# Norm weights and roots behind the transposes, and a dense gate and up with the rows stationary

## The reference

```python
h = rms_norm(x, attn_norm[i])             # x * rsqrt(mean(x^2) + eps) * gain
sb_q, sb_k, sb_v, df_q, df_k, df_v = split(h @ w_in[i])
sb = rms_norm(stick_breaking(sb_q, sb_k, sb_v), sb_out_norm[i])       # 8 heads of 64
df = rms_norm(differential(df_q, df_k, df_v) , diff_subln[i]) * (1 - lambda_init)   # 4 heads of 128
x = x + concat(sb, df) @ w_out[i]
h2 = rms_norm(x, ffn_norm[i])
x = x + (silu(h2 @ w_gate) * (h2 @ w_up)) @ w_down         # layer 0, 2816 hidden columns
x = x + moe(h2)                                            # layer 1, top 2 of 8 experts, 3584 each
return rms_norm(x, final_norm)                             # after both layers
```

## Time and profile before

| | us |
|---|---|
| median of three runs | 1455.23 |
| profiled execution, device time | 1451.91 |
| profiled execution, span | 1450.1 |
| PE busy | 1410.1 (97%) |
| DVE busy | 1128.7 (78%) |
| ACT busy | 932.1 (64%) |
| POOL busy | 47.9 (3%) |
| mean granted TensorE clock | 0.993 of full |

### The profile page before, as it was taken

The page is one execution under the profiler, slowest core; times in us unless marked ns, Lnnn a source line. Parts: engine busy times, 40 slices in busy tenths (PEclk is TensorE's granted clock), DMA queues, the critical chain, the costliest instruction groups (busy, mean ns, idle before and its releaser), DMA issues.

```text
span 1450.1 us, 19281 instructions
## 1 busy us (share of the span) xinstructions
PE 1410.1 (97%) x7417; PEld 1200.2 (83%) x7417; DVE 1128.7 (78%) x843; ACT 932.1 (64%) x742; POOL 47.9 (3%) x58
## 2 busy tenths in 40 slices
PE   7999999999999999999999999999999999999996
PEld 6877899988977788888888888888888888888885
DVE  5674554545674799988898898888888889889897
ACT  4454443434554577777777777777777777777775
POOL 0011000000011002000000000000000000000200
PEclk9999999999999999999999999999999999999999
DMA  8741796555542599999999999999999999999992
GB/s 307 258 146 58 282 354 222 183 194 162 172 146 62 199 356 395 393 398 394 389 376 392 384 365 384 394 357 397 383 370 387 382 380 373 385 397 357 396 395 104
DMA packets 190547, 450.61 MB, mean 311 GB/s; under 512 B 7529, under 2 KB 10638, under 8 KB 190494
## 3 DMA queue, kind: packets, MB, share of 16 engines
q1 hardware_dynamic: 188270, 442.43, 83.3%
q0 software_dynamic: 1936, 6.86, 1.3%
q10 hardware_dynamic: 288, 0.59, 0.1%
HBM read 431.49 MB, written 18.36 MB: 310 GB/s over the span
## 4 chain that ended last, share of the span: by engine, by line
PE 92%; DVE 3%; DMA 2%; ACT 1%; POOL 1%; SPq 1%; issue 0%; DVEq 0%
PE ps L511 86%; PE ps L852 2%; DMA raw<-in_w_in 1%; PE ps L608 1%; DVE hn L1178 1%; POOL hn L476 1%; DMA hn<-bias_scratch 1%; PE ps L632 0%; PE ps L810 0%; PE ps L655 0%; DVE aT_lo L1186 0%; DMA bias_scratch<-vrow 0%; DVE w_lo L350 0%; PE ps L821 0%; PE ps L597 0%
## 5 line engine op out<-in xcount | busy, mean ns | idle before, releaser
L350 DVE TENSOR_TENSOR w_lo<-raw,w_hi 128x2048 fp32r<-128x2048 f32 x401 | 914.9, 2291 | 208.9 <-ACT w_hi L345 208.1
L345 ACT ACTIVATE w_hi<-raw 128x2048 fp32r<-128x2048 f32 x401 | 768.0, 1917 | 314.4 <-PE ps L511 304.3
L511 PE MATMUL ps<-w_hi,xe_hi 128*128 128x512 f32 x896 | 244.7, 395 | 0.0
L511 PE MATMUL ps<-w_hi,xe_lo 128*128 128x512 f32 x896 | 240.0, 390 | 0.0
L511 PE MATMUL ps<-w_lo,xe_hi 128*128 128x512 f32 x896 | 239.9, 389 | 0.0
L511 PEld LDWEIGHTS ps<-w_hi,xe_lo 128*128 128x128 f32 x896 | 168.2, 188 | 35.9
L511 PEld LDWEIGHTS ps<-w_lo,xe_hi 128*128 128x128 f32 x896 | 168.2, 188 | 35.5
L511 PEld LDWEIGHTS ps<-w_hi,xe_hi 128*128 128x128 f32 x896 | 164.6, 188 | 31.6
L511 PE MATMUL ps<-w_hi,he_hi 128*128 128x512 f32 x448 | 120.6, 391 | 0.0
L511 PE MATMUL ps<-w_lo,he_hi 128*128 128x512 f32 x448 | 119.9, 389 | 0.0
L511 PE MATMUL ps<-w_hi,he_lo 128*128 128x512 f32 x448 | 119.8, 389 | 0.0
(11 more groups left out here) (220 smaller groups left out, 956.9 us busy)
## 6 DMA issues: line engine op xcount, KB each, us to landing
raw<-in_expert_w_gate SPq DMA_DIRECT2D x112, 1024.0 KB, 7.8
raw<-in_expert_w_up SPq DMA_DIRECT2D x112, 1024.0 KB, 8.0
raw<-in_expert_w_down SPq DMA_DIRECT2D x112, 1024.0 KB, 7.8
raw<-in_w_in SPq DMA_DIRECT2D x24, 1024.0 KB, 7.8
raw<-in_dense_w_gate SPq DMA_DIRECT2D x11, 1024.0 KB, 6.6
raw<-in_dense_w_up SPq DMA_DIRECT2D x11, 1024.0 KB, 8.2
raw<-in_dense_w_down SPq DMA_DIRECT2D x11, 1024.0 KB, 4.8
raw<-in_w_out SPq DMA_DIRECT2D x8, 1024.0 KB, 5.1
```

The source lines that it names most:

```text
L345: nc.scalar.activation(w_hi[:, n % SPL, :], raw[:, n % RAW, :], ACT.Copy).then_inc(hi_ready, 1)
L350: nc.vector.tensor_tensor(w_lo[:, n % SPL, :], raw[:, n % RAW, :], w_hi[:, n % SPL, :].bitcast(F32), ALU.subtract).then_inc(lo_ready, 1)
L511: return pe.matmul(o, stationary, moving, start=start, stop=stop, skip_group_check=True)
```

## The change

The transposes now read `xs`, the raw residual (`turn_x`). Its two halves of columns are added apart (`add_half`); the first half is turned before w_out's or down's last tile, the second behind it. Each column of the gain stands on a partition of the transposed copy (`gT`, itself transposed from the gain rows at the start), so ACT's copy and DVE's subtraction take it as their scale (`turned_x`, four operations of 128 x 256 a side for two of 128 x 512). The root of a row is applied to each product's output: to queries and keys through `rB` (the root spread over columns by one product with `diag`), to differential scores, values and the dense gate (as Silu's scale) and up by row. The head gains `gC` go the same way as `gT`; POOL's and DVE's multiplications of head rows go.

Dense gate and up go by rows, second half of the residual's columns last; the product of Silu and up is transposed on PE (`turn_dense`, 44 transposes) and copied as `hT_hi` and `hT_lo`. The router reads unscaled transposed rows, with `rw` times the gain (loaded at the start on SP's queue); the one-hot of the gather carries the root, and ACT scales the stored rows in the first expert block. The dummy matmuls of a run, 12, 9, 11, 9, 6 and 4 in the order of the program, become 8 and 16 at the start and 6, 6 and 4 in the router. Cut to its core:

```diff
-                sp.dma_start(g_sb[:].rearrange("p l d -> p (l d)"),
-                             sb_out_norm.rearrange("l d -> (l d)").partition_broadcast(P)).then_inc(small_in, 16)
-                sp.dma_start(g_df[:].rearrange("p l d -> p (l d)"),
-                             diff_subln.rearrange("l d -> (l d)").partition_broadcast(P)).then_inc(small_in, 16)
+                sp.dma_start(head_rows[0:DEPTH, 0:HD], sb_out_norm[:, :]).then_inc(small_in, 16)
+                sp.dma_start(head_rows[0:DEPTH, HD:2 * HD], sb_out_norm[:, :]).then_inc(small_in, 16)
+                sp.dma_start(head_rows[DEPTH:2 * DEPTH, :], diff_subln[:, :]).then_inc(small_in, 16)
+                sp.dma_start(rw[:], router_w[0].rearrange("(k p) e -> p k e", p=P)).then_inc(rw_in, 16)
...
-            norms = [attn_norm[0], ffn_norm[0], attn_norm[1], ffn_norm[1], final_norm]
-
-            def load_gain(m):
-                pool.wait_ge(rows_done[1], [None, 1, 3, 4, 6][m])
-                pool.dma_start(gain[:], norms[m].partition_broadcast(P)).then_inc(gain_in, 16)
-
+            pool.dma_start(gain[:], ffn_norm[DEPTH - 1].partition_broadcast(P)).then_inc(gain_in, 16)
...
-                pool.wait_ge(sbo_saved, l + 1)
-                pool.wait_ge(small_in, 16 * 2)
-                for t in range(TT):
-                    h = hn[:, t, 0:HALF].rearrange("p (h d) -> p h d", d=HD)
-                    nc.gpsimd.tensor_tensor(h, h, g_sb[:, l, :].unsqueeze(1).to_broadcast([P, SB_HEADS, HD]),
-                                            ALU.mult).then_inc(sb_rows, 1)
                 if l == 0:
-                    load_gain(2)
+                    pool.wait_ge(x_done[1], 1)
...
-            keep_running(12, 0)
+            keep_running(8, 0)
+            pe.wait_ge(norms_in, 32)
+            pe.transpose(ps[:, 3, 0:2 * DEPTH * KT], norm_rows[:], ident[0:2 * DEPTH * KT, 0:2 * DEPTH * KT]).then_inc(gT_turned, 1)
+            turn_x(0, (0, 1, 2, 3), 4)
+            keep_running(16, 0)
...
+                pe.wait_ge(diag_done, l + 1)
+                pe.matmul(ps[:, 6, 0:S], ones, diag[:].rearrange("p t k -> p (t k)"), start=True, stop=True,
+                          skip_group_check=True).then_inc(rB_spread, 1)
...
-                turn_rows(3 * l + 1, (0, 1), 6)
+                turn_rows((0, 1))
                 pe.wait_ge(t_lo, 12 * l + 8)
-                w_out(2)
-                w_out(3, ends=True)
-                keep_running(9, 6)
-                turn_rows(3 * l + 2)
+                w_out(2, ends=True)
+                w_out(3, (0,), ends=True)
+                turn_x(2 * l + 1, (0, 1))
+                w_out(3, (1,))
...
+                    def turn_dense(n):
+
+                        pe.wait_ge(hid_done, n + 1)
+                        width = CH if n < D_FULL else D_REST
+                        for f in range(width // P):
+                            for t in range(TT):
+                                last = pe.transpose(ps[:, 4 * (n % 2) + f // 2, (f % 2) * S + t * P:(f % 2) * S + t * P + P],
+                                                    hn[:, n % 2, t * width + f * P:t * width + f * P + P], ident)
+                        last.then_inc(hT_turned, 1)
...
+                        if n == 0:
+                            pe.wait_ge(t_lo, 10)
+                            rows_out(g, bank, 1, opens=1, tiles=(0,))
+                            turn_x(1, (2, 3))
+                            rows_out(g, bank, 1, opens=1, tiles=(1,))
+                            pe.wait_ge(t_lo, 12)
+                            rows_out(g + 1, bank, 0, opens=1)
+                        elif n < D_FULL:
+                            rows_out(g, bank, 1, opens=1)
+                            rows_out(g + 1, bank, 0, opens=1)
+                        else:
+                            rest_out(g, bank)
+                        if n > 0:
+                            turn_dense(n - 1)
                         if n < D_FULL:
-                            for half in range(2):
-                                if n == 0:
-                                    pe.wait_ge(t_lo, 10 + 2 * half)
-                                columns_out(g + half, bank, half)
-                            for half in range(2):
-                                columns_out(g + 2 + half, bank + 2, half)
+                            rows_out(g + 2, bank + 2, 1, opens=1)
+                            rows_out(g + 3, bank + 2, 0, opens=1)
                         else:
-                            columns_out(g, bank, 0, KT, D_REST)
-                            columns_out(g + 1, bank + 2, 0, KT, D_REST)
-                    for i in range(DENSE_DN):
-                        n = PROJ + WOUT + DENSE_GU + i
-                        hi = high(n)
-                        if i % 2 == 0:
-                            pe.wait_ge(hT_lo_done, i // 2 + 1)
+                            rest_out(g + 1, bank + 2)
...
+                            if (c, t) == (1, 1):
+                                turn_x(2, (0, 1))
+                            down_hi(DENSE_DN - 2, c, t)
+                            last = down_lo(DENSE_DN - 2, c, t)
...
+            pe.wait_ge(rw_ready, 1)
+            pe.wait_ge(rT_done, 2)
+            for k in range(4):
+                logits(k)
+            keep_running(6, 1)
+            turn_x(2 * DEPTH - 1, (2, 3))
+            pe.wait_ge(rT_done, 3)
+            for k in (4, 5):
+                logits(k)
+            pe.wait_ge(rT_last, 1)
+            logits(6)
+            logits(7).then_inc(lg_done, 1)
...
+            def turned_x(r, pairs, bank=6):
+
+                m, l = 2 * (r // 3) + r % 3 // 2, r // 3
+                for i, j in enumerate(pairs):
+                    act.wait_ge(t_done, 4 * r + j + 1)
+                    for q in range(2):
+                        k = 2 * j + q
+                        last = copy(aT_hi[:, x_slot(m, k), :], ps[:, bank + i, q * S:q * S + S], gT[:, DEPTH * (m % 2) + l, k:k + 1])
+                    last.then_inc(t_hi, 1)
...
-                    row_norms(0)
+                    act.wait_ge(gT_saved, 1)
+                    turned_x(0, (0, 1), 4)
                     split_hi(act, 0)
-                    turned(0)
+                    turned_x(0, (2, 3), 6)
                     split_hi(act, 1)
                     split_hi(act, 2)
+                    row_norms(0)
                 else:
+                    turned_x(3, (0, 1))
+                    split_hi(act, n0 + 1)
                     row_norms(2)
+                    turned_x(3, (2, 3))
                     split_hi(act, n0 + 2)
-                    turned(3 * l)
...
-                copy(both(v_sb[:]), both(ps[:, 0:2, :])).then_inc(v_sb_saved, 1)
-                turned(3 * l + 1, (2, 3), 6, 0)
+                act.wait_ge(r_done, 2 * l + 1)
+                for t in range(TT):
+                    last = copy(v_sb[:, t, :], ps[:, t, :], row_fine[:, t:t + 1])
+                last.then_inc(v_sb_saved, 1)
+                act.wait_ge(gC_saved, 1)
+                turned(3 * l + 1, (2, 3), gC[:, 1, l:l + 1])
...
+                    def silu(n):
+
+                        act.wait_ge(piece_used, min(PROJ + WOUT + 4 * n + 4, PROJ + WOUT + DENSE_GU))
+                        act.wait_ge(r_done, 2)
+                        for t in range(TT):
+                            at = slice(t * chunk(n) // TT, (t + 1) * chunk(n) // TT)
+                            last = nc.scalar.activation(hn[:, n % 2, at], both(ps[:, 4 * (n % 2):4 * (n % 2) + 2, :])[:, at],
+                                                        ACT.Silu, scale=row_fine[:, t:t + 1])
+                        last.then_inc(silu_done, 1)
...
+            def scale_rows():
+
+                act.wait_ge(ga_done, 2)
+                act.wait_ge(r_done, 4)
+                for t in range(TT):
+                    copy(hn[:, t, :], hn[:, t, :], row_fine[:, t:t + 1]).then_inc(rows_scaled, 1)
...
+            def low_part(out, source, gain_column, hi):
+                return V.scalar_tensor_tensor(out=out, in0=source, scalar=gain_column, in1=hi.bitcast(F32),
+                                              op0=ALU.mult, op1=ALU.subtract)
...
+                root(2 * l)
+                for t in range(TT):
+                    last = V.tensor_scalar(diag[:, t, :], ident, row_fine[:, t:t + 1], None, ALU.mult)
+                last.then_inc(diag_done, 1)
...
-                V.tensor_copy(both(qk_df[:, 4:8, :]), both(ps[:, 2:4, :])).then_inc(k_df_saved, 1)
+                V.tensor_tensor(qk_df[:, 4:8, :], four(ps[:, 2:4, :]), r_columns, ALU.mult).then_inc(k_df_saved, 1)
...
+                dve.wait_ge(piece_used, n0 + 6)
+                V.scalar_tensor_tensor(out=qk_sb[:, 0:4, :], in0=four(ps[:, 0:2, :]), scalar=HD ** -0.5, in1=r_columns,
+                                       op0=ALU.mult, op1=ALU.mult).then_inc(q_sb_saved, 1)
...
-                V.tensor_copy(both(v_df[:]), both(ps[:, 0:2, :])).then_inc(v_df_saved, 1)
```

(33 more changed lines are left out.)

484 lines of the change are left out of this document (302 added, 182 removed).

## The result

| | before | after |
|---|---|---|
| median, same chip, 5 runs each (us) | 1455.09 | 1461.96 |
| lowest to highest | 1453.42 to 1455.31 | 1460.3 to 1463.87 |
| profiled execution, span | 1450.1 | 1460.8 |
| PE busy | 1410.1 | 1434.2 |
| first expert product starts at | 488.7 | 475.3 |

The ratio is 1.0058, 95% interval 1.0045 to 1.0071: slower by 7 us, beyond the 0.2% that can be told. The forecast was faster by 18.7.

The account below looks back on a forecast made before the run. PE was taken to bound the kernel, with 92% of the chain of waits. The terms summed to -18.7 us, giving 1436.5, say 1437 us, against the 1455.2 us median; range 1430 to 1446 with (b), (c) and (d).

Parts of the forecast that it names:

- norm before dense: Between layer 0's w_out and the dense stage: the 7.3 us norm chain shrinks to 1.8 us of transposes, -5.5 us.
- dense to layer 1: Between dense stage and layer 1: the 8.1 us norm gap closes the same way, -6.3 us.
- head gains: Head norm in both layers: PE's transposes follow w_out without waiting for POOL's multiplication, 1.5 us a layer, -3.0 us.
- router: From w_out's end to the first expert product: new order shortens the path to the logits, -2.6 us together.
- dense stage: Dense gate and up by rows: -6.4 us from twenty full pieces, +5.0 for 44 transposes, together -1.4 us.
- clock: Slow PE restarts, 1.4 us each: the one before the dense stage and three quarters of the other go, -2.4 us.
- start: Kernel start: ACT's squares and root delay the fourth piece's split and `vrow`, +1.5 us, bounds -1 and +5.9.
- attention, root product: Attention values scaled by row, +0.6 us, and the product spreading the root over columns in layer 1, +0.4 us.
- (b): Rival at the start: it costs its upper bound, +5.9 us instead of +1.5, giving 1441 us; chance 0.12.
- (a): Rival in the dense stage: PE waits for hidden rows at six turns, slower at 1458 us; chance 0.04.
- (c): Rival at four places: the gaps close by half only, 7 us stay, giving 1444 us; chance 0.12.
- (d): Rival at the dense stage's turns: the clock falls, six restarts of 1.4 us cost 8.4, 1445 us; chance 0.06.

Follow-up runs that it names:

- same_place: Changed kernel plus an unused 1120-byte tile behind rw, putting aT, hT, xe and he at the addresses of the kernel before: 1433.08 us, ratio 0.9868.
- early_root: same_place with the first norm's squares ahead of piece 2's split on ACT, its root, diagonal and vrow copy ahead of the low split on DVE: 1428.9 us.

## Why the prediction was wrong

**The step that failed** is the sentence "The change touches the expert stage once and can gain nothing there", and the spacing of 2.72 us for twelve products that was carried over to all products after it. A spacing read from one kernel was taken for a property of the instruction. It is one of the instruction and of where its operands stand, and the change moved these by dropping two small tiles: twelve expert products took 2.80 us, and the expert stage got 24.1 us longer. No rival had it; "an expert stage that moved at all" stood only among the signs that would prove the forecast wrong, and this is what the profile showed. The miss is 25.6 us (18.7 + 6.9); after and same_place, which differ in nothing but the starts, are 25.4 us apart by the differences of their medians to before, and 27.6 by the ratios.

**The rest of the sum.** same_place runs the change with the operands at the distances of before, so its trace tests the other terms. Its PE at the end of layer 0's w_out, order of time (L593 turns the residual):

```profile
129.20 1.04 PE L577 MATMUL ps<-cst,hn 128*128 128x128 f32 x8
132.24 1.34 PE L512 MATMUL ps<-w_hi,aT_hi 128*128 128x512 f32 x4 [2.00 <-DVE aT_lo L1357]
...
142.15 1.03 PE L593 MATMUL ps<-cst,xs 128*128 128x128 f32 x8
142.94 1.17 PE L512 MATMUL ps<-w_hi,aT_hi 128*128 128x512 f32 x4
...
145.76 1.07 PE L512 MATMUL ps<-w_hi,aT_hi 128*128 128x512 f32 x4
...
148.50 1.04 PE L593 MATMUL ps<-cst,xs 128*128 128x128 f32 x8
149.29 1.17 PE L512 MATMUL ps<-w_hi,aT_hi 128*128 128x512 f32 x4
```

The gate's first product follows w_out's last at 145.76 without a wait, and each turn costs 0.79 us.

| term | forecast | same_place | how read |
|---|---|---|---|
| norm before dense | -5.5 | -5.7 | 7.3 to two turns of 0.79 |
| dense to layer 1 | -6.3 | -6.3 | 7.86 to two turns (329.36, 334.92) |
| head gains | -3.0 | -2.7 | 4.37 us between the two halves of w_out, now 3.04, in both layers |
| router | -2.6 | -2.2 | first expert product 17.6 us after w_out, now 14.6, and 0.8 inside w_out |
| dense stage | -1.4 | -1.1 | 188.2 to 185.7, 1.4 of it the clock |
| clock | -2.4 | +0.6 | see below |
| start | +1.5 | -1.2 | first products behind the bias at 46.54, before 47.77 |
| attention, root product | +1.0 | +1.3 | 82.2 to 82.7 in layer 0, 105.5 to 106.4 in layer 1 |
| sum | -18.7 | -17.3 | first expert product at 471.35, before 488.68 |

Every time here runs from the start of one group to the start of the next; for the last group before a wait, its start and the 0.91 us that four products are apart. The turns of the residual are counted with their norm or the router, not with the stage that they stand in. The median of same_place is 18.5 under that of before. That the sum came near is in part luck: two terms were wrong by about 3 us each, start and clock, and cancelled. The *start* was worked out with its waits right (ACT's split of the fourth piece came behind the squares, PE stood 3.2 us for `vrow`), but with the transfers wrong. The third piece landed at 21.6 and not at 23.96. The gain loads that went from the queues may be why; no run tested it. The start came out at the lower bound, -1; rival (b) went the other way. The chain of waits after:

```profile
10.44 11.19 DMA raw<-in_w_in
...
23.56 2.09 ACT hn L1040 x4
...
30.37 0.47 DVE vrow L1464
```

The third piece was in flight 11.19 us, before 13.65. The load of `rw`, made of short runs, ahead of it did no harm that can be seen, so the end of the range to which the Trainium skill (DMA: Bandwidth & Descriptors, Specifications) pointed wasn't reached.

The *clock*: the restart before the dense stage is gone as forecast (-1.4). Of the other, three quarters were counted as gone, and it stayed: 36 products took 9.91 us in layer 0 of same_place against 8.29 at full rate in the same place of early_root. In same_place the restart in layer 1, fast before, was slow too (9.92), which cost 1.7; layer 0 lost another 0.3. It differs from run to run of nearly the same program, so no term should have been made of it.

**The rivals.** (a) PE waiting for hidden rows: the turns inside the dense stage stand without a wait (after, order of time):

```profile
180.07 1.09 PE L511 MATMUL ps<-w_lo,aT_hi 128*128 128x512 f32 x4
181.00 1.03 PE L786 MATMUL ps<-cst,hn 128*128 128x128 f32 x8
181.79 0.48 PE L511 MATMUL ps<-w_hi,aT_hi 128*128 128x512 f32 x1
```

The result came out on its side, for another reason. (c) The gaps of the two norms closed whole. (d) No restart followed these turns: the 96 products between two of them take 21.8 us, eight times 2.72, in same_place. The rule of the Trainium skill that transposes don't count as activity (TensorE: Matmul & The Clock Gate, Part 4: PE-mode transpose) would have made (d) likelier; eight transposes among products did not bring it about here. The prediction said that the row of layer 1 doesn't contradict this rule; with the same transposes and a fast restart (11.21 us) that row speaks against it.

One slip in the prediction's working changes little: the router's steps add up to 6.6 us, not 6.8.

## What to carry to other kernels

A change that adds, drops or resizes any SBUF tile can change the rate of products that it doesn't touch; compare the spacing of untouched products in the two traces first, and list the operands' starts modulo 256 bytes before forecasting. To judge a change by itself, pad the changed kernel until its operands stand as before. And an address that is best for one form (rows at a distance of 0) isn't for another (columns at 192), so a comparison of two forms holds only for the distance it was made at.

## What the runs showed of the hardware

With the three products of a split float32 pair, 128x128 stationary and 512 columns moving, the spacing is 0.2272 us where the starts of stationary and moving operand are a multiple of 256 bytes apart (0 and 256 more were run), 0.229 at 192, and 0.232 to 0.234 at the six other distances seen (32, 64, 96, 128, 160, 224), a loss of 2.3 to 3.1%. At 160 it is the same with no DMA running and ACT and DVE at rest, so it needs no traffic of another engine; what causes it inside PE no run here shows. With 256 columns moving the order is another: 48 products in an unbroken run take 5.44 us at 192 and 5.76 at 0, 6% apart. Distances that aren't multiples of 32 bytes weren't tried.
